# A hybrid block with 32 routed experts on one core: the routed bias, the first result plane and the last visit are put elsewhere

## The reference

```python
logits = (xt @ w_router + b_router)
top_val, top_idx = lax.top_k(logits, 4)            # 4 of 32 experts for each token
gates = softmax(top_val)
hid = x_blk @ w_gate_up[e] + b_gate_up[e]          # 1024 -> 2048, for the tokens of expert e
gate, up = hid[:, :1024], hid[:, 1024:]
gate = minimum(gate, 7); up = clip(up, -7, 7)
act = (up + 1) * (gate * sigmoid(1.702 * gate))
yb = act @ w_down[e] + b_down[e]                   # 1024 -> 1024
y[token] += yb * row_gate                          # over the 4 experts of the token
out = rmsnorm(x + y)
```

## Time and profile before

| | us |
|---|---|
| median of 3 runs | 1393.46 (1392.11 to 1394.92) |
| the profiled execution | 1395.12 |
| its span, first to last instruction | 1393.3 |
| PE busy | 1235.3 (89%) |
| DVE busy | 681.9 (49%) |
| POOL busy | 325.3 (23%) |
| ACT busy | 220.4 (16%) |
| HBM read and written | 445.02 MB and 14.81 MB |

### The profile page before, as it was taken

How to read it: one execution, slowest core, us unless ns; L and a number is a source line. 1 busy time by engine, 2 the same in 40 slices (tenths; PEclk the granted TensorE clock), 3 DMA queues, 4 the chain that set the end, 5 groups by cost and what they waited for, 6 DMA issues and landing times.

```text
span 1393.3 us, 32055 instructions
## 1 busy us (share of the span) xinstructions
PE 1235.3 (89%) x12818; PEld 541.6 (39%) x12819; DVE 681.9 (49%) x1365; ACT 220.4 (16%) x435; POOL 325.3 (23%) x435
## 2 busy tenths in 40 slices
PE   6999999999599999899899999787987887879992
PEld 3444554564234443344433334233332332333331
DVE  2898884444644364335434333435443334354428
ACT  3124543412100011000110000000110000001103
POOL 6001111010222233222323312222233222222221
PEclk9999999999799999999999999999999999999995
DMA  9212000311589999999999999999999999999996
GB/s 303 91 60 91 1 31 1 160 65 78 217 343 404 404 421 421 426 426 428 425 424 424 425 426 426 425 425 426 427 423 426 426 426 425 426 426 425 385 407 250
DMA packets 58142, 455.33 MB, mean 327 GB/s; under 512 B 12060, under 2 KB 22356, under 8 KB 32982
## 3 DMA queue, kind: packets, MB, share of 16 engines
q1 hardware_dynamic: 44660, 434.13, 75.3%
q0 software_dynamic: 11664, 18.95, 3.8%
q10 hardware_dynamic: 1778, 1.69, 0.5%
HBM read 445.02 MB, written 14.81 MB: 330 GB/s over the span
## 4 chain that ended last, share of the span: by engine, by line
PE 53%; DMA 35%; DVE 7%; issue 2%; ACT 2%; POOL 0%; SPq 0%; POOLq 0%; DVEq 0%; ACTq 0%
DMA ring<-in_w_gate_up_dram 24%; PE bank L2165 22%; PE bank L2218 11%; DMA dslots<-in_w_down_dram 10%; PE bank L1825 6%; PE bank L2016 4%; DVE dslots L1144 3%; PE bank L1820 2%; DVE hbuf L1719 1%; PE bank L1893 1%; PE bank L1900 1%; DMA wq<-xn_rows,idx_in 1%; DMA rows<-in_x_dram 1%; PE bank L2151 1%; PE bank L1981 1%
## 5 line engine op out<-in xcount | busy, mean ns | idle before, releaser
L2165 PE MATMUL bank<-ring,wq 128*32 128x512 f32 x4992 | 561.2, 599 | 66.7 <-DMA ring<-in_w_gate_up_dram 63.9
L2165 PEld LDWEIGHTS bank<-ring,wq 128*32 128x32 f32 x4992 | 167.5, 110 | 420.1 <-issue 417.5
L2218 PE MATMUL bank<-dslots,intra 128*32 128x256 f32 x5056 | 281.7, 380 | 26.5 <-DMA dslots<-in_w_down_dram 26.2
L2218 PEld LDWEIGHTS bank<-dslots,intra 128*32 128x32 f32 x5056 | 165.8, 110 | 152.5 <-issue 55.9
L1532 DVE TENSOR_REDUCE small<-bank 128x4 f32<-128x8 f32 x33 | 5.5, 166 | 416.0 <-PE bank L2129 416.0
L1011 ACT ACTIVATE zrows<-intra 128x1024 f32<-128x1024 f32 x31 | 32.8, 1058 | 794.0 <-DVE intra L1625 794.0
L1825 PE MATMUL bank<-hbuf,ring 128*128 128x512 f32 x320 | 148.5, 604 | 0.2 <-ACT hbuf L752 0.2
L618 POOL COPY idx_in<-idx 128x4 int32 (+1 forms) x32 | 11.9, 371 | 555.2 <-DVE wq L1510 533.3
L623 POOL DMA_INDIRECT wq<-xn_rows,idx_in x82 | 101.8, 1241 | 44.2 <-POOL idx_in L618 27.8
L1597 DVE STREAM_TRANSPOSE wq<-bank 128x512 f32<-128x512 f32 x124 | 77.8, 685 | 68.5 <-PE bank L2165 68.5
L628 POOL DMA_INDIRECT y_rows<-rows,idx_out x79 | 81.2, 1027 | 55.7 <-issue 43.6
(11 more groups left out here) (302 smaller groups left out, 900.0 us busy)
## 6 DMA issues: line engine op xcount, KB each, us to landing
ring<-in_w_gate_up_dram SPq DMA_DIRECT2D x127, 2048.0 KB, 25.0
dslots<-in_w_down_dram SPq DMA_DIRECT2D x61, 2048.0 KB, 25.4
ring<-in_w_in_dram SPq DMA_DIRECT2D x12, 1024.0 KB, 12.7
ring<-in_w_out_dram SPq DMA_DIRECT2D x4, 1024.0 KB, 4.9
ring<-in_w_down_dram SPq DMA_DIRECT2D x4, 1024.0 KB, 24.8
dslots<-y_rows SPq DMA_DIRECT2D x2, 2048.0 KB, 20.2
rows<-in_x_dram SPq DMA_DIRECT2D x4, 512.0 KB, 9.4
hbuf<-in_x_dram SPq DMA_DIRECT2D x4, 512.0 KB, 5.4
```

The costliest lines, as they stand in the source:

```text
L2165: ins = M(bank[g][GROUP * j:GROUP * (j + 1), :], x[:, g, c * GROUP:(c + 1) * GROUP], w[:, :, j * QD:(j + 1) * QD], start=(c == 0), stop=(c ...
L2218: ins = M(b[GROUP * j:GROUP * (j + 1), col:col + QD], actT[:, g, c * GROUP:(c + 1) * GROUP], w[:, cc, j * QD:(j + 1) * QD], start=(c == 0 ...
```

## The change

Three edits that belong together.

1. `routed_bias` and `gates_turn` leave the last visit and go to visit 16 (`MID`). The loops of PE, ACT and DVE are cut in two there. In visit 16 PE takes pair 0, bias 0, pair 2, bias 1, pair 4, bias 2, pair 6, bias 3, waits for the last addition, does the small index product of line 2129 and then the older down product. b_down is loaded into `ffnw` instead of `qkbuf`, which comes free.
2. Plane 0 is loaded by SP before pair 4 of expert 31, in two halves, into `convbuf` and `qkbuf`. DVE adds it before `last_act`, no longer after it. Planes 1 and 2 go to the upper half of `ring` and plane 3 to `dslots`.
3. In the last visit PE takes the four chunk pairs in a row and then the down product of expert 30. SP loads in the same order: pair 4, pair 6, and then the two halves of expert 30's down weights, which stood ahead of them. The last activation writes to `qkbuf` (`actT_last`) instead of `intra`, so it need not wait for the older down product. ACT does the last sigmoids before the results of expert 30. The second of the last expert's four down loads now waits for the scatter of expert 29.

The diff, cut to its core:

```diff
--- before.py
+++ after.py
@@ -34,6 +34,7 @@
+MID = 16
@@ -212,7 +213,7 @@
...
         GT = vbuf[0:E, :]
-        bdn = qkbuf[0:E, 0:D]
+        bdn = ffnw[0:E, :]
         ab_sb = thbuf[:, 0:SEQ]
...
@@ -225,12 +226,13 @@
...
         actT = view(intra, CAP * 8, GROUPS, KC * GROUP)
+        actT_last = view(qkbuf, 0, GROUPS, KC * GROUP)
         yb = view(rows, 0, GROUPS, QD)
...
         fin = view(hbuf, 0, T, D)
-        PLANES = [view(dslots, 0, T, D), view(dslots, 2 * SLOT, T, D), view(ring, 4 * SLOT, T, D),
-                  view(ring, 6 * SLOT, T, D)]
+        PLANES = [None, view(ring, 4 * SLOT, T, D), view(ring, 6 * SLOT, T, D), view(dslots, 0, T, D)]
+        FIRST_PLANE = [view(convbuf, 0, 2, D), view(qkbuf, 0, 2, D)]
...
@@ -442,25 +444,27 @@
...
+            def plane(k):
+                return y_dram[k * NR_ROWS:(k + 1) * NR_ROWS, :].rearrange("(t p) d -> p t d", p=P)
             for c in range(0, KC, 2):
                 if c == 4:
-                    for u in (0, 2):
-                        sp.wait_ge(d_used, m * 4 + (u + 2))
-                        down_pair(None, u)
+                    sp.wait_ge(landed, m * 16 + 16)
+                    for half in range(2):
+                        sp.dma_start(FIRST_PLANE[half], plane(0)[:, 2 * half:2 * half + 2, :]).then_inc(plane_in[0], 16)
                 sp.wait_ge(gu_used, m * KC + (c + 2))
                 gate_up(E - 1, c)
+            for u in (0, 2):
+                sp.wait_ge(d_used, m * 4 + (u + 2))
+                down_pair(None, u)
             for u in range(4):
-                sp.wait_ge(gu_used, m * KC + (KC + u + 1))
+                if u % 2 == 0:
+                    sp.wait_ge(gu_used, m * KC + (KC + u + 2))
+                if u == 1:
+                    sp.wait_ge(landed, m * 16 + 32)
                 sp.dma_start(view(ring, u * SLOT, 2, D), down_rows(E - 1, u)).then_inc(slot_in[u], 16)
-            def plane(k):
-                return y_dram[k * NR_ROWS:(k + 1) * NR_ROWS, :].rearrange("(t p) d -> p t d", p=P)
-            sp.wait_ge(d_used, m * 4 + 8)
-            sp.dma_start(PLANES[0], plane(0)).then_inc(plane_in[0], 16)
-            sp.wait_ge(landed, m * 16 + 16)
+            sp.wait_ge(gu_used, m * KC + (KC + 6))
             sp.dma_start(PLANES[1], plane(1)).then_inc(plane_in[1], 16)
...
@@ -662,7 +666,7 @@
...
             m = visits_less_two(pool)
-            pool.sem_inc(landed, 16)
+            pool.sem_inc(landed, 32)
             pool.wait_ge(idx_ready, 3)
...
@@ -994,8 +998,8 @@
+            act.wait_ge(route_ready, 1)
             act.dma_start(bdn, b_down[0]).then_inc(bias_in, 16)
-            act.wait_ge(route_ready, 1)
             m = visits_less_two(act)
@@ -1013,19 +1017,24 @@
...
             sigmoid_gate(1)
-            with act.Fori(1, m + 1) as i:
+            def visit(i):
                 sigmoid_gate(i + 1)
                 act.wait_ge(d_used, i * 4 + 4)
-                act.wait_ge(landed, i * 16)
+                act.wait_ge(landed, i * 16 + 16)
                 results((i - 1) % STAGES)
+            with act.Fori(1, MID) as i:
+                visit(i)
             act.wait_ge(gt_done, 1)
             A(GT, bank[7][0:E, :], ACT.Copy).then_inc(gt_copied, 1)
-            act.wait_ge(d_used, m * 4 + 8)
-            act.wait_ge(landed, m * 16 + 16)
-            results((E - 2) % STAGES)
+            with act.Fori(MID, m + 1) as i:
+                visit(i)
             for g in range(GROUPS):
...
                 A(sg[:, g, :], g2[:, g, :], ACT.Sigmoid, scale=ALPHA).then_inc(sg_last, 1)
+            act.wait_ge(d_used, m * 4 + 8)
+            act.wait_ge(landed, m * 16 + 32)
+            results((E - 2) % STAGES)
             for g in range(GROUPS):
...
@@ -1641,8 +1650,7 @@
...
             own.n += STEPS_ACT
-            with dve.Fori(1, m + 1) as i:
-                base = (i - 1) * LOOP_OWN + own.n
+            def rows_ahead(i, base):
                 dve.wait_ge(idx_done, i + 3)
...
@@ -1651,9 +1659,25 @@
...
                 lower(e3)
+            def visit(i):
+                base = (i - 1) * LOOP_OWN + own.n
+                rows_ahead(i, base)
                 hid_turn(i + 1)
...
                 act_part(i % E, i + 1, base + STEPS_IDX)
+            with dve.Fori(1, MID) as i:
+                visit(i)
+            base = (MID - 1) * LOOP_OWN + own.n
+            for t in range(T):
+                add_bias(t)
+            hid_turn(MID + 1)
+            rows_ahead(MID, base)
+            xt_turn(MID + 1)
+            act_part(MID, MID + 1, base + STEPS_IDX)
+            with dve.Fori(MID + 1, m + 1) as i:
+                visit(i)
...
@@ -1694,7 +1718,7 @@
...
                     after(k)
-                    V.scalar_tensor_tensor(out=actT[:, g, :], in0=u2[:, g, :], scalar=1.0, in1=g2[:, g, :],
+                    V.scalar_tensor_tensor(out=actT_last[:, g, :], in0=u2[:, g, :], scalar=1.0, in1=g2[:, g, :],
                                            op0=ALU.add, op1=ALU.mult).then_inc(act_last, 1)
@@ -1704,14 +1728,14 @@
...
+            dve.wait_ge(plane_in[0], 32)
+            dve.wait_ge(acc_ready, T)
             for t in range(T):
-                add_bias(t)
+                V.tensor_tensor(fin[:, t, :], fin[:, t, :], FIRST_PLANE[t // 2][:, t % 2, :], ALU.add).then_inc(added, 1)
             dve.wait_ge(gu_used, m * KC + 2 * KC)
-            dve.wait_ge(d_used, m * 4 + 4)
             last_act()
-            dve.wait_ge(acc_ready, T)
-            for k in range(TOP_K - 1):
+            for k in range(1, TOP_K - 1):
                 dve.wait_ge(plane_in[k], 16)
...
@@ -2238,28 +2262,35 @@
...
             gate_up(0, first=True, known=tokens)
-            with pe.Fori(1, m + 1) as i:
-                pe.wait_ge(xt_ready, i + 2)
-                gate_up(i)
+            def older_down(i):
                 pe.wait_ge(act_ready, i)
...
                 down(i - 1, tokens)
+            def visit(i):
+                pe.wait_ge(xt_ready, i + 2)
+                gate_up(i)
+                older_down(i)
+            with pe.Fori(1, MID) as i:
+                visit(i)
+            tokens = tokens_left(pe, MID)
+            pe.wait_ge(xt_ready, MID + 2)
+            pe.wait_ge(idx_ready, MID + 2)
+            gates_turn()
+            for t in range(T):
+                gate_up(MID, pairs=(2 * t,), known=tokens)
+                routed_bias(t)
+            pe.wait_ge(acc_ready, T)
+            idx_mm(MID + 2, (MID + 3) * (T + 1) - 1)
+            older_down(MID)
+            with pe.Fori(MID + 1, m + 1) as i:
+                visit(i)
             tokens = tokens_left(pe, m + 1)
             pe.wait_ge(xt_ready, m + 3)
-            pe.wait_ge(idx_ready, m + 3)
-            gates_turn()
-            gate_up(m + 1, pairs=(0,), known=tokens)
-            routed_bias(0)
-            gate_up(m + 1, pairs=(2,), known=tokens)
-            routed_bias(1)
-            pe.wait_ge(act_ready, m + 1)
-            pe.wait_ge(y_ready, m + 1)
-            down(m, tokens_left(pe, m))
-            routed_bias(2)
-            gate_up(m + 1, pairs=(4,), known=tokens)
-            routed_bias(3)
-            gate_up(m + 1, pairs=(6,), known=tokens)
+            gate_up(m + 1, known=tokens)
+            older_down(m + 1)
...
@@ -2267,7 +2298,7 @@
...
                         ins = M(bank[g][GROUP * j:GROUP * (j + 1), 0:QD],
-                                actT[:, g, c * GROUP:(c + 1) * GROUP],
+                                actT_last[:, g, c * GROUP:(c + 1) * GROUP],
                                 w[:, cc, j * QD:(j + 1) * QD], start=(c == 0), stop=(c == KC - 1))
...
```

## The result

| | before | changed |
|---|---|---|
| median of 13 runs each | 1394.16 us (1392.11 to 1397.50) | 1399.23 us (1395.79 to 1402.39) |
| ratio to before | | 1.003 [1.002, 1.004] |
| profiled execution | 1395.12 | 1399.01 |
| its span | 1393.3 | 1397.3 |
| second series of the changed kernel (11 runs) | 1393.52 | 1396.60, ratio 1.0021 [1.0012, 1.0030] |

The change made the kernel slower by 0.2 to 0.3%, about 3 to 5 us. The loss is small, but both intervals lie clear of 1, and the forecast was no measurable change. In the profiled execution the forecast of 1396.1 was 2.9 us too low; of the two medians, the first lies just above the stated range (1398.5), the second inside it.

The account below looks back on a forecast made before the run. Weight loads were taken as the bound, with PE, load queue and DVE's planes ending within two microseconds. +0.7 + 0.3 + 0 = 1.0 us on 1395.12 gave 1396.1 profiled, 1394.5 as median; 8-in-10 range 1390.5 to 1398.5.

Parts of the forecast that it names:

- +0.7 for plane 2: End of the kernel: plane 2 lands late, so DVE begins the last plane's addition 0.7 us later than 1379.41.
- +0.3 for the clock: Last visit: PE's 6.4 us stall ahead of pair 4 may lower its clock; 0.3 us put on it.
- 0 for visit 16: Visit 16: 9.5 us of added PE work and waiting fit into idle time, counted as nothing.
- The load queue sets the last visit: Last visit: loads land in turn, 5.19 us per 2 MB; the 8.2 us saved on PE are all spent waiting.
- End of the older down product, 1356.8: Last visit: PE ends expert 30's down product at 1356.8, 12.6 us later than before.
- From there to plane 2's issue, 11.6 us: After expert 30's down product: scaling, scatter and issue of plane 2 take 11.6 us as before, giving 1368.4.
- Plane 2's landing, 7.1 us with ends 6.5 and 7.8: Plane 2's load starts on an empty queue, takes 7.1 us (6.5 to 7.8) and lands at 1375.5.
- The last plane is 3 us early: End: PE ends at 1366.1, last plane issued at 1373.4, first tile by 1376.8, 3 us before DVE wants it.
- tail of 13.9 us: From the start of the last plane's addition to the end of the kernel: 13.9 us as before.
- the faster queue: Rival, chance 0.12: loads at the end are faster, plane 2 lands at 1370.2; 4.2 us less, 1389.3.
- PE as the bound: Rival, chance 0.06: TensorE was the bound, so the removed 8.2 us come off whole, about 1385.3.
- The clock: Rival, chance 0.14: gaps leave PE at 1.2 GHz through expert 30's down product; 1397.1 to 1399.5, say 1398.3.

Follow-up runs that it names:

- bias_only: Kernel before with only the bias products moved to visit 16, last visit and planes as before; ratio to before 0.9997, tail 98.1 us.
- norm_early: Changed kernel with the load of the final norm weights moved from the end to visit 16; ratio to before 1.0020, tail 100.5 us.
- plane_behind: Changed kernel with the early load of plane 0 moved behind expert 30's down weights; ratio to before 1.0066, tail 106.0 us.
- plane2_tiles: Changed kernel with plane 2 loaded as four tiles with a semaphore each; ratio to before 1.0011, tail 99.5 us.
- old_order: Changed kernel with the last visit in the old order, plane 0 loaded early behind expert 30's down weights; ratio to before 1.0000, tail 97.3 us.
- plane2_unbound: Changed kernel whose plane 2 load reads plane 0's rows without waiting for expert 30's scatter; ratio to before 0.9993, tail 97.2 us.

## Why the prediction was right and where it missed

The sum had three terms. The +0.7 for plane 2 measured 4.0: DVE began the last plane at 1383.39 instead of 1379.41. The +0.3 for the clock was not on the path that ended last, and the 0 for visit 16 held. So the mechanism was right, the size of its main term was not, and the direction (slower) was in the forecast only as 1.0 us.

- **The load queue sets the last visit**: right. Pair 0 of expert 31 landed at 1321.1 (1295.92 + 25.2). PE waited for the first of expert 30's down loads until 1346.9; the second landed at 1351.7, six units after pair 0 as computed (predicted 1351.3 from 1320.2), and PE is not seen to wait for it. The 8.2 us saved on PE all went into waiting.
- **Visit 16 costs nothing**: right (bias_only, 1.01 DMA share in its window).
- **End of the older down product, 1356.8**: 3.3 us too early. Some 0.9 came with pair 0. Pairs 4 and 6 took 8.86 us instead of 7.2 (the granted clock is 0.59 from 1337.5 to 1342.0, so at 1.2 GHz for most of it, and 1.00 after that), but they ended at 1346.4 and PE then still waited 0.56 us for the down load, so this cost the product nothing. The rest are two pauses of 0.79 and 0.98 us inside the product, put down to "issue", and some 0.8 us by which its three pieces together take longer than one. Before there was none; every kernel built from the changed one has them. In all of these PE waits for a load in the last visit, and in all of them the loops are cut at visit 16, so which of the two brings the pauses is open.
- **From there to plane 2's issue, 11.6 us**: it took 7.9 (1360.1 to 1367.95). The queue was nearly empty, and plane 2 went out 1.7 us after POOL's last issue for expert 30 (1366.24), where it had been 5.4 us (1350.36 to 1355.74). That the two errors cancelled is luck: issue at 1367.95, predicted 1368.4.
- **Plane 2's landing, 7.1 us with ends 6.5 and 7.8**: this term failed. It took 10.9 us, and 9.9 in the second series. I had priced it on an empty queue from the last plane, but at 1370.4 ACT issues the norm weights and at 1369.4 to 1373.6 POOL the last scatter, and they share the sixteen engines. Before, ACT's load was issued at 1368.8 and the scatter from 1369.5 on, when plane 2 (landed at 1372.1) was nearly through. norm_early shows 1.2 to 2.2 us of it for the norm weights. No run has plane 2 alone on an empty queue, so the 7.1 us itself is shown by none; the shortest landing behind the gap was 8.4 us, in plane_behind.
- **The last plane is 3 us early**: wrong in size. PE ended at 1368.3 instead of 1366.1, and the scatter, beside plane 2, took 6.8 us to land instead of 3.3; the issue came at 1378.99, not 1373.4, and the first tile 1.1 us before DVE wanted it. The tail of 13.9 us was right.
- **Rivals**: the faster queue and PE as the bound did not happen. The clock cost something, 1.7 us in pairs 4 and 6, but not in the down product. The side that came true, slower, I had at 0.22, for other reasons: the price came from the step of my own forecast. That the measured time still lies near the range owes something to a range that was made wide for those other reasons.

## What to carry to other kernels

When a stream of loads is the bound, moving compute off the last stage buys only waiting; ask which load needs the result of the work that was moved back, and write its issue time down beside the queue's. The loss here lay in a queue that ran more than half empty for 14 us (share 0.44), and in a late load that then had to share the engines with two others; it took two edits together, each harmless alone, to bring it about. A path that ends 1 us behind the last one should be written down too: it caps what any cure of the first can give. A load "on an empty queue" must be priced with every other queue's loads of those microseconds, and a reordered step with what now stands ahead of it on each engine, as plane_behind showed on ACT.

## What was not expected of the hardware

A 2 MB load took 25.2 us from issue to landing in the full stream, 9.9 to 10.9 beside a 0.5 MB load and a scatter, and 8.4 to 8.7 without the former; 2 MB in turn in the queue cost 5.0 to 5.3. The last expert's scatter took 6.1 to 6.8 us to land where plane 2 had been issued just ahead of it (the changed kernel twice, norm_early, plane2_tiles), and 3.0 to 3.5 where plane 2 was nearly through (before, old_order, plane2_unbound). The mean DMA share can fall without making the landings late: in 1355 to 1360 and 1360 to 1365 of the changed kernel it was 0.66 and 0.41, and plane 1 still came in its turn by 1366.8. Why was not tried. Straight-line matmul code of the same shape ran without a pause when PE had come to it busy (10.57 us for 192) and with two pauses of 0.3 to 1.1 us in the kernels in which PE waited for loads in that visit, all of which also have their loops cut.
